# A two-block mixer kernel in one launch: where the last delta-rule head gets its gate products, and three waits around it

## The reference

```
h = rms_norm(x)
gu,gv,gz, rq,rk,rv,rz, dq,dk,dv,dz, a_f,b_f,a_b,b_b = split(h @ w_in)
y_a = gmlp(gu, gv) * silu(gz)
y_b = retention(rq, rk, rv) * silu(rz)
y_c = gdn(silu(conv(dq,dk,dv)), a, b) * silu(dz)     # 4 heads of width 128
proj  = einsum(branches, w_branch_out)               # 3 branches
gates = sigmoid(h @ w_gate)
x = x + sum(gates * proj) @ w_out
```

## Time and profile before

| | |
|---|---|
| median of 3 runs | 2603.8 us (2602.19 to 2604.39) |
| the profiled execution | 2603.8 us |
| its span, first to last instruction | 2602.0 us, so 1.8 us lie around it |
| PE busy | 2552.3 us, 98% of the span |
| POOL, ACT, DVE busy | 51%, 41%, 40% |
| mean granted TensorE clock | 0.997 of 2.4 GHz |

### The profile page before, as it was taken

One profiled execution on the slowest core, in us unless ns is written; L12 is line 12 of the kernel. 1 busy time (PEld: TensorE's weight loads), 2 busy tenths in 40 slices (PEclk: granted clock), 3 DMA queues, 4 the chain that ended last, 5 costly groups with the idle time before them and its releaser, 6 DMA issues.

```text
span 2602.0 us, 36414 instructions
## 1 busy us (share of the span) xinstructions
PE 2552.3 (98%) x12788; PEld 2049.7 (79%) x12788; DVE 1034.8 (40%) x2185; ACT 1062.3 (41%) x1642; POOL 1327.1 (51%) x1016
## 2 busy tenths in 40 slices
PE   9999999999999999999999999999999989999999
PEld 7878888888778788888876478888887746888887
DVE  6567442114575653113666632111014584211100
ACT  6336443235526344224546433333234463333321
POOL 6424755567633665556742125666556212566653
PEclk9999999999999999999999999999999999999999
DMA  5212113334222212333321113333333101333332
GB/s 195 84 49 82 47 37 96 95 95 131 81 65 66 66 42 65 96 95 125 106 82 33 33 51 95 97 97 97 97 109 118 49 25 54 93 96 96 95 100 73
DMA packets 62366, 215.12 MB, mean 83 GB/s; under 512 B 7312, under 2 KB 10512, under 8 KB 61840
## 3 DMA queue, kind: packets, MB, share of 16 engines
q1 hardware_dynamic: 62224, 213.28, 26.8%
HBM read 211.16 MB, written 2.10 MB: 82 GB/s over the span
## 4 chain that ended last, share of the span: by engine, by line
PE 77%; issue 11%; POOL 8%; DVE 3%; ACT 1%; POOLq 0%; ACTq 0%; DVEq 0%
PE bank L839 19%; PE bank L841 19%; PE bank L840 19%; POOL wl L2388 6%; PE pair L839 2%; PE pair L841 2%; PE pair L840 2%; PE pair L1610 2%; PE bank L1569 1%; PE bank L1570 1%; PE bank L1592 1%; POOL hl L2434 1%; PE pair L1423 1%; PE pair L849 1%; DVE soft L3309 1%
## 5 line engine op out<-in xcount | busy, mean ns | idle before, releaser
L2388 POOL TENSOR_TENSOR wl<-raw,wh 128x512 fp32r<-128x512 f32 x766 | 1021.3, 1356 | 1144.0 <-ACT wh L2019 378.4
L839 PE MATMUL bank<-hh,wh 128*128 128x512 f32 x1600 | 633.0, 396 | 0.0
L841 PE MATMUL bank<-hh,wl 128*128 128x512 f32 x1600 | 623.8, 390 | 0.0
L840 PE MATMUL bank<-hl,wh 128*128 128x512 f32 x1600 | 623.5, 390 | 0.0
L841 PEld LDWEIGHTS bank<-hh,wl 128*128 128x128 f32 x1600 | 300.4, 188 | 63.1
L839 PEld LDWEIGHTS bank<-hh,wh 128*128 128x128 f32 x1600 | 300.7, 188 | 60.5 <-issue 0.5
L840 PEld LDWEIGHTS bank<-hl,wh 128*128 128x128 f32 x1600 | 300.7, 188 | 59.8 <-issue 0.5
L2339 ACT CAST wh<-raw 128x1024 fp32r<-128x1024 f32 x120 | 125.4, 1047 | 254.1 <-PE pair L841 140.3
L1780 ACT CAST wh<-raw 128x1024 fp32r<-128x1024 f32 x104 | 109.0, 1049 | 131.9 <-PE bank L841 97.3
L839 PE MATMUL bank<-wh,hh 128*128 128x512 f32 (+2 forms) x352 | 138.9, 395 | 3.0 <-ACT vg L1799 1.6
L2019 ACT CAST wh<-raw 128x1024 fp32r<-128x1024 f32 x84 | 86.9, 1049 | 128.2 <-PE bank L841 108.8
(11 more groups left out here) (459 smaller groups left out, 4650.7 us busy)
## 6 DMA issues: line engine op xcount, KB each, us to landing
raw<-stream SPq DMA_DIRECT2D x384, 512.0 KB, 3.6
mraw<-memin SPq DMA_DIRECT2D x3, 1024.0 KB, 5.6
par<-params SPq DMA_DIRECT2D x2, 1124.5 KB, 8.8
out<-xT SPq DMA_DIRECT2D x8, 256.0 KB, 2.0
con<-consts SPq DMA_DIRECT2D x1, 1540.0 KB, 14.8
xT<-xin SPq DMA_DIRECT2D x2, 512.0 KB, 4.6
xT<-xin SPq DMA_DIRECT2D x1, 1024.0 KB, 8.4
con<-consts SPq DMA_DIRECT2D x1, 512.0 KB, 3.1
```

What stands on the lines that cost most here:

```text
L839: mm(o, ah, bh, start=start, stop=False)
L840: mm(o, ah, bl, start=False, stop=False)
L841: return mm(o, al, bh, start=False, stop=stop)
L2388: m = TT(wl[slot][:, c], raw[slot][:, c], wh[slot][:, c].bitcast(F32), ALU.subtract)
```

## The change

On PE, `front(0)` waits for `vtok_ready` 4 ahead of its transposes, in place of 3 behind them and 4 ahead of `halves(0, 0)`. On ACT, `hi(g + 4)` of granules 32 to 35 stands ahead of the `vtok` copy.

In head 3 only granule 42 is used for filling, its 8 parts spread over the places of all 16: 3, 1, 1, 1, 1 ahead of the `v_new` products, the eighth behind them, none in the steps st = 1 to 3. The state of direction 0 then goes to bank 5 (`state_bank`). Granule 43 is done after the head, in bank 7: four parts, `head_sums(3)`, four parts, `head_spread(3)`. ACT follows: `hi(46)` behind `gate_z(6, 7)` and ahead of the `v_new` copies, `head_root(3)`, `gate_z(7, 7)` and `hi(47)` behind the head. The three branches are one loop on PE, gate tile e in bank e%4, and the waits for `proj_taken` 44 and `yc_raw` 4 stand at the loop's head.

```diff
                 def front(h):
                     if h == 0:
+                        wait("vtok_ready", 4)
                         wait("proj_taken", 35)
...
-                    else:
-                        wait("vtok_ready", 3)
...
-                    gate_part(36 + 2 * h, 7, range(4))
+                    near = 4 if h < H - 1 else 3
+                    gate_part(36 + 2 * h, 7, range(near))
                     if h:
                         head_sums(h - 1)
-                    gate_part(36 + 2 * h, 7, range(4, 6))
+                    gate_part(36 + 2 * h, 7, range(near, near + 2 if h < H - 1 else near + 1))
                     if h == 0:
                         wait("proj_taken", 36)
-                        wait("vtok_ready", 4)
                     halves(h, 0)
...
+                    if h < H - 1:
+                        gate_part(37 + 2 * h, 5, range(4, 5))
+                    else:
+                        gate_part(36 + 2 * h, 7, range(7, 8))
                     states(0)
                     for st in range(1, NT):
-                        gate_part(37 + 2 * h, 5, range(4 + st, 5 + st))
+                        if h < H - 1:
+                            gate_part(37 + 2 * h, 5, range(4 + st, 5 + st))
...
-                def branch(n, between):
+                wait("proj_taken", 43)
+                gate_part(43, 7, range(4))
+                head_sums(H - 1)
+                gate_part(43, 7, range(4, KD))
+                head_spread(H - 1)
+
+                with pe.Fori(0, 3) as n:
...
                     pe.wait_ge(s["gate_taken"].sem, B * 8)
+                    wait("proj_taken", 44)
+                    wait("yc_raw", 4)
...
-                branch(0, {0: head_sums, 1: head_spread})
-                with pe.Fori(1, 3) as n:
-                    branch(n, {})
...
+                    hi(g + 4)
                     wait("vt_done", z + 1)
                     inc(A(vtok[z]...), "vtok_ready")
-                    hi(g + 4)
...
                     gate_z(2 * h, 7)
+                    if h == H - 1:
+                        hi(40 + 2 * h)
                     for st in range(NT):
...
+                head_root(H - 1)
+                gate_z(2 * H - 1, 7)
+                hi(39 + 2 * H)
```

More of the change, by code:

```diff
@@ L1113, in chunk_scores, with state_bank @@
                     inc(m, "kq_done")
+                def state_bank(h, d):
+                    return 6 if d else 7 if h < H - 1 else 5
                 half_ps = [bk[3][:, 0:P].rearrange("p (c n) -> p c n", c=NT), bk[3][:, P:3 * P].rearrange("p (c n) -> p c n", c=NT)]
@@ L1177, in _ @@
                     halves(h, 1)
-                    gate_part(37 + 2 * h, 5, range(2))
+                    if h < H - 1:
+                        gate_part(37 + 2 * h, 5, range(2))
+                    else:
+                        gate_part(36 + 2 * h, 7, range(5, 6))
                     new_blocks(h, 1)
-                    gate_part(37 + 2 * h, 5, range(2, 4))
+                    if h < H - 1:
+                        gate_part(37 + 2 * h, 5, range(2, 4))
+                    else:
+                        gate_part(36 + 2 * h, 7, range(6, 7))
                     chunk = lambda st, d: st if d == 0 else NT - 1 - st
@@ L1195, in states @@
                                 wait("rhs_ready", 5 * h + d + 4)
-                                if d == 0:
+                                if d == 0 and h < H - 1:
                                     wait("proj_taken", 37 + 2 * h)
@@ L1199, in states @@
                                     wait("yc_raw", h)
-                            inc(mm(b4[7 - d][:, st], KDT[d][:, c], VNEW[d][st % 2], start=True, stop=True), "s_done")
+                            inc(mm(b4[state_bank(h, d)][:, st], KDT[d][:, c], VNEW[d][st % 2], start=True, stop=True), "s_done")
                     for d in range(2):
@@ L1207, in _ @@
                         inc(mm(b4[1 + d][:, c], Y[d][:, c], BV[:, c], start=True, stop=True), "vn_done")
-                    gate_part(37 + 2 * h, 5, range(4, 5))
+                    if h < H - 1:
+                        gate_part(37 + 2 * h, 5, range(4, 5))
+                    else:
+                        gate_part(36 + 2 * h, 7, range(7, 8))
                     states(0)
                     for st in range(1, NT):
-                        gate_part(37 + 2 * h, 5, range(4 + st, 5 + st))
+                        if h < H - 1:
+                            gate_part(37 + 2 * h, 5, range(4 + st, 5 + st))
                         for d in range(2):
@@ L1245, in gate_tile @@
                             pe.wait_ge(s["gate_taken"].sem, B * 8 + e - 3)
-                        elif e == 3:
-                            wait("go_sq", H)
                         w = g % SLOTS
                         for k in range(KD):
-                            m = three(bk[(e + 1) % 4], wh[w][:, k * P:(k + 1) * P], wl[w][:, k * P:(k + 1) * P],
+                            m = three(bk[e % 4], wh[w][:, k * P:(k + 1) * P], wl[w][:, k * P:(k + 1) * P],
                                       hh[:, k], hl[:, k], k == 0, k == KD - 1)
@@ L1262, in branch_tiles @@
                                 pe.wait_ge(s["merged"].sem, B * 8)
-                                wait("proj_taken", 44)
-                                wait("yc_raw", 4)
                             for k in range(H):
@@ L1950, in _ @@
                             inc(A(VNEW[d][st % 2], b4[1 + d][:, c], ACT.Copy), "vn_ready")
-                    gate_z(2 * h + 1, 5)
+                    if h < H - 1:
+                        gate_z(2 * h + 1, 5)
                     wait("out_done", 8 * h + 8)
@@ L1968, in hi_n @@
                         nc.scalar.copy(wh[g % SLOTS][:, :], raw[g % SLOTS][:, :]).then_inc(hi_ready, 1)
[L1970 to L1973, removed]
+                    wait("y_gated", 8)
                     act.wait_ge(granule_done, G + n * 12 + G_PROJ)
@@ L1986, in branch @@
                                 act.wait_ge(s["merged"].sem, B * 8)
-                            A(gs[e][:, :], bk[(e + 1) % 4], ACT.Sigmoid).then_inc(s["gate_taken"].sem, 1)
+                            A(gs[e][:, :], bk[e], ACT.Sigmoid).then_inc(s["gate_taken"].sem, 1)
                             hi_n(6 * q + e + 4)
-                            if (n, j) == (0, 0):
-                                head_root(H - 1)
                         if last and q == 1:
@@ L1998, in branch @@
                                 hi_n(6 * q + 4 + f + 4)
-                for n in range(3):
-                    branch(n, n == 2)
+                with act.Fori(0, 2) as n:
+                    branch(n, False)
+                branch(2, True)
                 for e in range(KD):
```

13 lines of the change are left out of this document (7 added, 6 removed).

## The result

| | before | after |
|---|---|---|
| median of 5 runs each, us | 2603.8 (2602.19 to 2605.27) | 2619.16 (2618.17 to 2619.59) |
| ratio, with 95% interval | | 1.0057 [1.0045, 1.0069] |
| span of the profiled execution, us | 2602.0 | 2617.2 |
| mean granted clock | 0.997 | 0.995 |

The change costs 15.4 us (11.7 to 18.0 by the interval). The direction was forecast; the size was not: 2612.1 was said, +8.3 us, and 2619.2 lies outside 2605.5 to 2617.5.

The account below looks back on a forecast made before the run. The prediction took PE's matmul queue, its waits and its granted clock, to bound the kernel. Per layer -0.63 + 4.85 + 1.15 = +5.37, twice +10.7, with -3.9 and +1.5 for the clock: +8.3, 2612.1 us; range 2605.5 to 2617.5.

Parts of the forecast that it names:

- entry without the clock: Entry into head 0: X comes 0.63 us earlier, PE's new wait falls into the old one's slack; -0.63 us per layer.
- head 3 (steps 1 to 5): Head 3: 5.55 us of matmuls leave, the head gets only 0.7 us shorter; +4.85 us per layer.
- clock in head 3: Head 3, behind PE's wait of about 2.3 us: half a low phase charged, 0.75 us per layer, +1.5 us in sum.
- The clock there: Entry into head 0: no clock fall behind the new 2.5 us wait, both layers' low-clock cost gone; -3.9 us in sum.
- The other bound of that step: Entry into head 0: clock falls all the same, a low phase loses 1.7 us per layer; -0.5 us in sum.
- Steps 1 to 4: Head 3 to its state products: 2.3 us gained, lost again waiting for ACT's v_new copies; state products at 375.98, before 375.92.
- Step 5: Head 3, steps st = 1 to 3: without gate parts each comes only 0.2 to 0.25 us earlier; 0.7 us in sum.
- Behind head 3: Loop's head after head 3: PE waits for head_scale, which gate tiles 2 and 3 covered before; +1.15 us per layer.
- Rival 3: Entry and head 3: the clock falls at both new waits, the skill's rule; +15.0 us, 2618.8 us, chance 0.15.
- Rival 1: Head 3 is bound by PE's queue, not the chain, so the 5.55 us come back; 2600.9 us, chance 0.08.
- Rival 2: Head 3: silu and cast don't hold the v_new copies, so the 2.3 us gain stays; 2605.9 us, chance 0.10.
- Rival 4: In and behind head 3: table loads start only once their granule is done; +12.1 us in all, 2615.9 us, chance 0.12.

Follow-up runs that it names:

- steps_bare: Kernel before with the last three parts of granule 43 moved from steps st = 1 to 3 to behind head 3; 2608.95 us, 1.0017.
- after_filled: Changed kernel with thrown-away matmuls filling PE's waits for vtok and ahead of head 3's state products; 2615.65 us, 1.0045.
- copies_first: Changed kernel with ACT's silu of bank 7 and cast of granule 46 behind head 3's first two v_new copies; 2612.25 us, 1.0031.
- entry_only: Kernel before with only the change at the entry into head 0 (ACT's order and PE's wait for vtok); 2602.62 us, 0.9994.
- swap_only: Kernel before with only ACT's cast put ahead of the vtok copy, PE's waits as before; 2603.43 us, 0.9997.
- swap_parts: Kernel before with ACT's cast ahead of the vtok copy and all eight parts of granule 36 ahead of halves(0, 0); 2606.7 us, 1.001.

## Why the prediction was wrong in size

Step by step, per layer. "Measured" is from stretches of the table and of the experiments, low phases as means over the profiles.

| term | forecast | measured |
|---|---|---|
| entry without the clock | -0.63 | -0.53 |
| clock at the entry | -1.95 | -0.7 |
| head 3 (steps 1 to 5) | +4.85 | +5.1 |
| wait behind it | +1.15 | +1.4 |
| clock in head 3 | +0.75 | +1.1 |
| sum of a layer | +4.17 | +6.4 |

**The step that failed is "The clock there".** It took both low phases of the entry as gone, on the ground that a wait of 2.5 us was nearer to one that had left the clock up. In the twelve layers profiled here with the wait of 2.5 us, the clock fell in six. In the eight profiled with before's wait of 3.45 us it fell in seven, three times for 6.8 us. In the mean the entry costs 1.18 us of clock with the old wait (21.59 - 20.41) and 0.46 with the new (20.34 - 19.88): 0.7 gained, not 1.95. That is 2.5 us of the miss of 7.1. There were two errors in it. The size: comparing head 0 with head 1 gave 1.46 and 2.40 us, whereas the same stretch with and without a low phase gives 1.0 and 1.9. Head 0 is the longer one even at full clock: in the second execution of before, where the clock stayed up in layer 0, it takes 3.95 us from `halves(0, 0)` to `chunk_scores` and not 3.46, with a wait of 0.38 us for POOL's `Y` (at 281.13) that head 1 has not and that a low clock hides. And the probability: a thing that happens half of the time was entered as not happening. The other bound of that step erred the other way: it took a low phase of 3.4 us to cost 1.7, where 0.9 to 1.0 is measured.

**"The clock in head 3"** had the right mechanism and too small a size: half a low phase, 0.75, where the clock fell in seven of eight layers with that wait, at 1.3 us each: 1.1. It fell in none of four when the copies came first, and in neither layer when the wait was filled.

**Steps 1 to 4** hold to 0.1 us (from the head's first transpose: `halves` 5.92, spread 8.20, `v_new` products 14.87, state products 18.26, against 5.94, 8.24, 14.8 and 18.27). Step 5 counted 0.7 us won back over three steps; steps_bare, as the experiment is called, shows 0.15. In the changed kernel the head became 0.3 us shorter instead of 0.7 (28.50 us from its first transpose in layer 1, where the clock stayed up, forecast 28.1, before 28.80). **Behind head 3** the wait was 1.4 with what overlaps, for 1.15. ACT there, in layer 0 after:

```profile
390.62 1.28 ACT L1937 ACT_TABLE_LOAD   x1 [2.68 <-PE pair L1100]
391.92 0.26 ACT L1937 ACTIVATE root<-pair,eps_b 128x4 f32<-128x4 f32 x1
392.33 1.28 ACT L1932 ACT_TABLE_LOAD   x1
393.62 0.60 ACT L1932 ACTIVATE zs<-pair 128x512 f32<-128x512 f32 x1
```

The load for the root starts only when `head_sums` is done, so its 1.28 us lie in the chain, but the reciprocal is done at 392.46, 0.8 us ahead of the spread. The silu starts as its load ends (393.61) and is over at 394.22, ahead of `head_scale` (394.68), which PE waits for. Root and silu start 1.30 and 1.29 us after the start of their load. The drain of 1380 ns that the Trainium skill ("ScalarE: Activation LUTs", What ACT_TABLE_LOAD costs) adds to a load does not show.

**Rival 3**, the clock falling at both new waits, gave 2618.8, and 2619.2 was measured. It was right in kind: the clock falls behind the new waits as it did behind the old one. But the number is luck. The clock fell at 13 of 20 such waits, and where the rival charged +4.3 us for the clock in sum, the table above has +0.8 (two layers of -0.7 and +1.1). Of the Trainium skill's rule ("TensorE: Matmul & The Clock Gate", HAM oscillation) the runs bear out that a wait in a stream of matmuls can be paid twice; after_filled shows it directly. But here the return is not paid at each wait: the clock fell in one execution and not in the next. Rival 1 (head bound by PE) fell: even with the order of ACT mended the head gave back 2.0 of 5.45 us. Rival 2 fell, since the copies were held; what the holding costs copies_first measures as 6.9 us, for 6.2 by the rival's terms, but in other shares (3.5 of waiting and 2.2 of clock in place of 4.7 and 1.5). Rival 4 fell: head 3's table load is done at 370.51, two microseconds ahead of the silu, whose granule ends last.

Of the prediction's own signs of being wrong, one came true: the clock fell at a place where none was forecast, the entry.

**What stays open.** Two layers of 6.4 make 12.7 us; 15.4 were measured, with 12.7 inside the interval of 11.7 to 18.0. The table seems to put the missing part in the second block, where this change edits nothing: 1.7 us on average of two profiles each. All unfilled profiles together don't bear this out. The three stretches of block 2 sum to 126.1 to 129.8 us, mean 128.0, in the six of kernels that keep the fillers ahead of head 3's state products (before twice, entry_only, swap_only, swap_parts, steps_bare), and to 126.1 to 129.8, mean 128.1, in the six with the changed head 3. Low phases there scatter by up to 3.7 us from profile to profile, whichever head 3 the kernel has. Where the missing 2.7 us come from stays open, and they may be noise.

No version here is clearly faster than the kernel before: the best two, 0.9994 and 0.9992, have 1 in their intervals.

## What to carry to other kernels

Matmuls that fill the waits of a latency chain are not free to move: of 5.45 us taken out of a head, 3.4 were lost with the best order tried. Up to the state products what was lost could be read beforehand from how far behind each filler the chain's next result lay; in the steps behind them that reading was too hopeful (0.7 us forecast, 0.15 to 0.3 measured). When work leaves an engine that runs in order, look at what is now *ahead* of the chain's copies in the queue of the others: here one silu and one cast that used to be early cost 1.75 us of waiting per layer, and 1.1 of clock behind it. Price a wait of PE like those here, 2.0 to 3.5 us long, with its low phase, times how often it falls, and take both from several profiles, not from one.

## What the runs showed of the hardware

- The granted clock is not a function of the program. With waits, shapes and addresses the same, it fell at the layer-0 entry in one execution of each of the two kernels and not in the other.
- Low phases inside the program lasted 3.4 or 6.8 us in all fourteen profiles. One of 3.4 us cost 0.9 to 1.0 us at the entry, 1.2 to 1.4 in head 3 and 1.5 in the dense matmuls of block 2, less than half its length each time.
- A wait of 2.0 us later in the program (block 2, for DVE's `tok`, at about 2099 us in before) had a low phase behind it in 11 of the 14 profiles, none in the first one of before, where the wait was 1.90 us.
- The clock also fell where PE had not waited: about 1270 us into the program, behind 28 matmul rows with an output of 128x1 (3.1 us), in one of the two executions of the kernel before and in 12 of the 14 profiles. In order of time (second execution of before):

```profile
1268.44 1.03 PE L849 MATMUL pair<-con,ssb 128*128 128x1 f32 x8
1269.34 0.46 PE L839 MATMUL bank<-wh,hh 128*128 128x448 f32 x1
...
1270.22 0.57 PE L839 MATMUL bank<-wh,hh 128*128 128x448 f32 x1
```

  PE has no bracket there, and the matmul of 448 columns, 0.36 us long at full clock, takes 0.57.
